# Dense products that read their moving operand, and write their bank, from the last column to the first

## The reference

```
mod = silu(c) @ w_ada + b_ada                       # 2048 x 6144, for the latent and for the context
u   = rms_norm(h) * (1 + scale) + shift             # 256 + 256 tokens
p   = u @ w_in                                      # z, x B C, dt, q k v, beta, alpha
y   = [ssd_scan(conv(xBC)), gdn_scan(conv(qkv))]    # both directions, context state carried to the latent
x   = x + gate * rms_norm(norm_gate(y) @ w_out)
for l in 0, 1:
    h = rms_norm(x); q k v b c i = split(h @ w_in_2[l])          # 2048 x 6144
    x = x + [diff_attention(q, k, v), b * conv3(c * i)] @ w_out_2[l]
    h = rms_norm(x)
    x = x + relu(h @ w_up_2[l])**2 @ w_down_2[l]                 # 2048 x 8192, 8192 x 2048
```

## Time and profile before

| | |
|---|---|
| time, median of 3 runs | 3028.11 us |
| time of the profiled execution | 3026.63 us |
| its span, first to last instruction | 3024.8 us |
| mean granted TensorE clock | 0.995 |
| TensorE matmul (PE) busy | 2981.0 us, 99% |
| weight load (PEld) busy | 2823.5 us, 93% |
| VectorE, ScalarE, GpSimd busy | 62%, 44%, 10% |
| DMA, mean | 181 GB/s |

### The profile page before, as it was taken

The page is one execution under the profiler, slowest core; times in us unless marked ns, Lnnn a source line. Parts: engine busy times, 40 slices in busy tenths (PEclk is TensorE's granted clock), DMA queues, the critical chain, the costliest instruction groups (busy, mean ns, idle before and its releaser), DMA issues.

```text
span 3024.8 us, 68274 instructions
## 1 busy us (share of the span) xinstructions
PE 2981.0 (99%) x28670; PEld 2823.5 (93%) x28670; DVE 1863.7 (62%) x2510; ACT 1333.8 (44%) x1732; POOL 295.3 (10%) x351
## 2 busy tenths in 40 slices
PE   6999999999999999999999999999999999999999
PEld 2688888888989999999999999999999999999999
DVE  3677777688876666555455555566665555555554
ACT  3455455455454444444343333444444443333333
POOL 0000000000111212110010000211122110000000
PEclk8999999999999999999999999999999999999999
DMA  9612212323955454555555555544545555555554
GB/s 398 276 58 85 85 60 83 122 101 113 394 184 203 180 178 174 190 195 192 191 191 192 193 193 195 222 177 172 180 173 189 192 191 191 191 193 193 195 194 153
DMA packets 82964, 547.13 MB, mean 181 GB/s; under 512 B 9125, under 2 KB 13365, under 8 KB 18928
## 3 DMA queue, kind: packets, MB, share of 16 engines
q1 hardware_dynamic: 78448, 523.27, 47.5%
q10 hardware_dynamic: 2192, 15.40, 1.3%
q0 software_dynamic: 2160, 6.05, 0.6%
HBM read 540.46 MB, written 7.36 MB: 181 GB/s over the span
## 4 chain that ended last, share of the span: by engine, by line
PE 95%; DMA 1%; DVE 1%; ACT 1%; PEld 0%; issue 0%; PEldq 0%; POOL 0%; SPq 0%; ACTq 0%; DVEq 0%; POOLq 0%
PE bank L446 29%; PE bank L447 28%; PE bank L448 28%; PE bank L864 1%; DMA raw<-stream 1%; PE bank L731 1%; PE bank L737 1%; PE bank L967 1%; DMA xr<-x_t 1%; PE bank L773 0%; PE bank L950 0%; PE bank L789 0%; PE bank L975 0%; PE bank L1179 0%; DVE rs L1726 0%
## 5 line engine op out<-in xcount | busy, mean ns | idle before, releaser
L425 ACT CAST w_hi<-raw 128x2048 fp32r<-128x2048 f32 x443 | 846.9, 1912 | 1222.0 <-PE bank L448 1221.9
L430 DVE TENSOR_TENSOR w_lo<-raw,w_hi 128x2048 fp32r<-128x2048 f32 x443 | 1020.1, 2303 | 549.5 <-ACT w_hi L425 549.2
L446 PE MATMUL bank<-a_lo,w_hi 128*128 128x256 f32 (+1 forms) x3568 | 1060.3, 297 | 0.5 <-PEq L459 0.3
L447 PE MATMUL bank<-a_hi,w_lo 128*128 128x256 f32 (+1 forms) x3568 | 1034.9, 290 | 0.0
L448 PE MATMUL bank<-a_hi,w_hi 128*128 128x256 f32 (+1 forms) x3568 | 1034.6, 290 | 0.0
L446 PE MATMUL bank<-h_lo,w_hi 128*128 128x256 f32 x3552 | 990.0, 279 | 3.8 <-DVE h_lo L2136 3.8
L447 PE MATMUL bank<-h_hi,w_lo 128*128 128x256 f32 x3552 | 981.5, 276 | 0.0
L448 PE MATMUL bank<-h_hi,w_hi 128*128 128x256 f32 x3552 | 981.4, 276 | 0.0
L446 PEld LDWEIGHTS bank<-a_lo,w_hi 128*128 128x128 f32 x3568 | 672.2, 188 | 24.6 <-DVE g_X L1906 2.7
L448 PEld LDWEIGHTS bank<-a_hi,w_hi 128*128 128x128 f32 x3568 | 670.1, 188 | 17.1
L447 PEld LDWEIGHTS bank<-a_hi,w_lo 128*128 128x128 f32 x3568 | 671.3, 188 | 12.2
(11 more groups left out here) (360 smaller groups left out, 2273.8 us busy)
## 6 DMA issues: line engine op xcount, KB each, us to landing
raw<-stream SPq DMA_DIRECT2D x485, 1024.0 KB, 4.8
gate_raw<-stream ACTq DMA_DIRECT2D x12, 1024.0 KB, 7.9
xr<-x_t SPq DMA_DIRECT2D x4, 1024.0 KB, 16.3
q_raw<-stream SPq DMA_DIRECT2D x8, 512.0 KB, 9.6
x_res<-x_t SPq DMA_DIRECT2D x1, 2048.0 KB, 16.6
bias_table<-bias SPq DMA_DIRECT2D x1, 2048.0 KB, 11.1
bias<-bias_table ACTq DMA_DIRECT2D x1, 2048.0 KB, 11.2
out_t<-x_res SPq DMA_DIRECT2D x4, 512.0 KB, 5.0
```

The source lines that it names most:

```text
L425: act.copy(w_hi[u.slot][:], raw[u.raw][:]).then_inc(hi_ready, 1)
L430: dve.tensor_tensor(w_lo[u.slot][:], raw[u.raw][:], w_hi[u.slot][:], ALU.subtract).then_inc(lo_ready, 1)
L446: pe.matmul(acc, wh, lo[:, k, 0:n], start=(k == first), stop=False)
L447: pe.matmul(acc, wl, hi[:, k, 0:n], start=False, stop=False)
```

## The change

`unit_mm` and the quarters of the small unit hand TensorE their moving operand and their bank through `backward`, an access pattern that begins at the last of the n columns and steps by -1. Column j of the operand still meets column j of the bank; the weights, their loads, the order of the matmuls and every wait are as before. The constants `U_SKEW`, `A_SKEW` and `H_SKEW`, all 192 bytes, replace `SKEW`, and name a place for each layer's operands; with these values every operand of a layer has the address it had. Three other things move: the spare weight tiles and the two `gate_raw` buffers that share their place begin 320 bytes later, at a multiple of 512, and `cs` (the 32 columns of silu(c), written once) goes to the end of the arena.

```diff
-SKEW = 48
+U_SKEW = 192
+A_SKEW = (192, 192)
+H_SKEW = (192, 192, 192, 192)
...
-        gate_raw = [put(f"gate_raw{k}", D, at=4 * (RAW * D + 2 * SPL * D + SKEW + KT * T + KT * L + k * D)) for k in range(2)]
+        gate_raw = [put(f"gate_raw{k}", D, at=X_RES - 4 * (2 - k) * D) for k in range(2)]
         for w, g in ((w_hi, 0), (w_lo, 1)):
-            w.append(put(f"w_spare{g}", D, F32R, at=4 * (RAW * D + 2 * SPL * D + SKEW + KT * T + KT * L + g * D)))
+            w.append(put(f"w_spare{g}", D, F32R, at=X_RES - 4 * (2 - g) * D))
...
+        def backward(x):
+
+            (step, rows), (one, n) = x.ap
+            return bass.AP(x.tensor, x.offset + (n - 1) * one, [[step, rows], [-one, n]])
+
...
-            acc = psum[u.bank][:, 0:n]
+            acc = backward(psum[u.bank][:, 0:n])
...
-                pe.matmul(acc, wh, lo[:, k, 0:n], start=(k == first), stop=False)
-                pe.matmul(acc, wl, hi[:, k, 0:n], start=False, stop=False)
-                last = pe.matmul(acc, wh, hi[:, k, 0:n], start=False, stop=(k == final))
+                xl, xh = backward(lo[:, k, 0:n]), backward(hi[:, k, 0:n])
+                pe.matmul(acc, wh, xl, start=(k == first), stop=False)
+                pe.matmul(acc, wl, xh, start=False, stop=False)
+                last = pe.matmul(acc, wh, xh, start=False, stop=(k == final))
...
-                acc = psum[u.bank][:, 0:n]
+                acc = backward(psum[u.bank][:, 0:n])
...
-                    pe.matmul(acc, wh, u_lo3[:, k, 0:n], start=(k == 0), stop=False)
-                    pe.matmul(acc, wl, u_hi3[:, k, 0:n], start=False, stop=False)
-                    last = pe.matmul(acc, wh, u_hi3[:, k, 0:n], start=False, stop=(k == KT - 1))
+                    xl, xh = backward(u_lo3[:, k, 0:n]), backward(u_hi3[:, k, 0:n])
+                    pe.matmul(acc, wh, xl, start=(k == 0), stop=False)
+                    pe.matmul(acc, wl, xh, start=False, stop=False)
+                    last = pe.matmul(acc, wh, xh, start=False, stop=(k == KT - 1))
```

More of the change, by code:

```diff
@@ L268, in build @@
         w_lo = [put(f"w_lo{s}", D, F32R) for s in range(SPL)]
[L269 to L273, removed]
+        A0 = top["at"]
+        u_hi, u_lo = (put(n, KT * T, F32R, at=A0 + U_SKEW + 4 * KT * T * k) for k, n in enumerate(("u_hi", "u_lo")))
+        a_hi, a_lo = ([put(n, KT * T, F32R, at=A0 + skew + 4 * KT * T * k) for skew in A_SKEW] for k, n in enumerate(("a_hi", "a_lo")))
+        top["at"] += 4 * (P + 2 * KT * T)
+        cs = put("cs", 2 * KT, at=4 * (53200 - T - HALF - 2 * KT))
         X_RES = top["at"]
@@ L354, in build @@
         top["at"] = shared
-        h_hi = put("h_hi", KT * L, F32R)
-        h_lo = put("h_lo", KT * L, F32R)
+        H0 = shared - 192
+        h_hi, h_lo = ([put(n, KT * L, F32R, at=H0 + max(skew, 192 + (skew - 192) % 512) + 4 * KT * L * k) for skew in H_SKEW]
+                      for k, n in enumerate(("h_hi", "h_lo")))
+        top["at"] += 4 * 2 * KT * L + max((skew - 192) % 512 for skew in H_SKEW)
         mo = put("mo", KT * L, at=shared + 4 * KT * L)
-        bias = put("bias", 2 * HEADS * L, at=4 * (RAW * D + 2 * SPL * D + SKEW + KT * L))
+        bias = [put("bias", 2 * HEADS * L, at=A0 + skew + 4 * KT * L) for skew in A_SKEW]
         n_sq, n_acc, n_ln, n_rs = (put(n, L) for n in ("n_sq", "n_acc", "n_ln", "n_rs"))
@@ L445, in unit_mm, with mixed3, normed3 @@
                 wh, wl = (w[u.slot][:, k * P:(k + 1) * P] for w in (w_hi, w_lo))
[L446 to L448 removed]
+                xl, xh = backward(lo[:, k, 0:n]), backward(hi[:, k, 0:n])
+                pe.matmul(acc, wh, xl, start=(k == first), stop=False)
+                pe.matmul(acc, wl, xh, start=False, stop=False)
+                last = pe.matmul(acc, wh, xh, start=False, stop=(k == final))
             if part[1] == KT:
                 last.then_inc(unit_done, 1)
[L452 to L454 removed]
+        u_hi3, u_lo3 = (a[:].rearrange("p (k t) -> p k t", t=T) for a in (u_hi, u_lo))
+        def mixed3(l):
+            return (a[l][:, 0:KT * L].rearrange("p (k t) -> p k t", t=L) for a in (a_hi, a_lo))
+        def normed3(m):
+            return (a[m][:].rearrange("p (k t) -> p k t", t=L) for a in (h_hi, h_lo))
         def leave(eng, k):
@@ L1577, in weighted_hi @@
                 tile = ds(i * (4 * L) + j * L, L)
-                act.mul(h_hi[:, tile], x_res[:, tile], par(name, i * 4 + (l * KT + j))).then_inc(S["h_hi_ready"], 1)
+                act.mul(h_hi[m][:, tile], x_res[:, tile], par(name, i * 4 + (l * KT + j))).then_inc(S["h_hi_ready"], 1)
             norm_root(0)
@@ L1675, in turn_ @@
                             tile = i * (4 * L) + ((q % 2) * KT + j) * L
-                            act.copy(a_hi[:, ds(tile, L)], hbuf[:, (2 + j % 2) * L:(3 + j % 2) * L]).then_inc(S["hi_relu"], 1)
+                            act.copy(a_hi[l][:, ds(tile, L)], hbuf[:, (2 + j % 2) * L:(3 + j % 2) * L]).then_inc(S["hi_relu"], 1)
                         elif not isinstance(i, int) or u.c + i * 4 + 2 < N_SEQ:
@@ L2135, in weighted_lo @@
                 tile = ds(i * (4 * L) + j * L, L)
-                stt(h_lo[:, tile], x_res[:, tile], par(name, i * 4 + (l * KT + j)), h_hi[:, tile], ALU.mult, ALU.subtract
+                stt(h_lo[m][:, tile], x_res[:, tile], par(name, i * 4 + (l * KT + j)), h_hi[m][:, tile], ALU.mult, ALU.subtract
                     ).then_inc(S["h_ready2"], 1)
@@ L2275, in turn_ @@
                             tile = ds(i * (4 * L) + ((q % 2) * KT + j) * L, L)
-                            tt(a_lo[:, tile], hbuf[:, (2 + j % 2) * L:(3 + j % 2) * L], a_hi[:, tile], ALU.subtract
+                            tt(a_lo[l][:, tile], hbuf[:, (2 + j % 2) * L:(3 + j % 2) * L], a_hi[l][:, tile], ALU.subtract
                                ).then_inc(S["mlp_ready"], 1)
```

31 lines of the change are left out of this document (17 added, 14 removed).

## The result

The changed kernel takes 3109.93 us, the median of 4 runs (3109.29 to 3111.96), against 3028.10 us of the kernel before, run beside it (4 runs, 3028.07 to 3029.24). The ratio is 1.027, with an interval from 1.026 to 1.0285. The profiled execution took 3110.09 us, its span is 3108.3 us, 83.5 us more than before. The forecast of 2985 us had the wrong sign; the time lies in the range of 2950 to 3140 only because the range had room for the first rival.

The account below looks back on a forecast made before the run. TensorE's instruction spacings were taken to bound the kernel. Gains of 16.9 + 8.4 + 7.1 + 9.7 + 0.7 = 42.8 us off 3026.6 gave 2983.8, forecast as 2985 us, with an 8-in-10 range of 2950 to 3140.

Parts of the forecast that it names:

- the first rival: All stages: slower because reads side by side are worse, +76 to +123 us; slower in all or part had chance 0.31.
- the moving read of 256 columns: Dense 256-column matmuls: spacing would become 112.4 ns, between the load's own 111.4 and today's best rhythm.
- The term for MLPs and projections: MLPs and projections: 16,896 matmuls going from 113.4 to 112.4 ns, 16.9 us faster.
- w_out_2: Stage `w_out_2`: 1,536 matmuls going from 117.9 to 112.4 ns, 8.4 us faster.
- First layer: First layer: 1,968 matmuls, from a middle of 116 ns, gaining 3.6 ns each, 7.1 us faster.
- 512 columns: Matmuls of 512 columns: half of a 15 ns excess goes from 1,296 of them, 9.7 us faster.
- Bank backward: Bank written from the last column: one column a cycle either way, cost 0.
- the rival of half rate: All dense matmuls: a negative step keeps read or write from one column a cycle, 5.3 ms slower; chance 0.06.
- Spare weights: Spare-weight units: 192 matmuls from 120 to 112.4 ns, 1.5 us, 0.7 of it not counted in other stages.
- side by side is worse: All stages at 117.9 or 120 ns, about 3104 to 3151 us; slower in all or part had chance 0.31.
- the rival of no change: All stages: direction is nothing, only 1 us from the spare weights, 3027 us; within 6 us, chance 0.15.
- The bound of failure: MLPs and projections: the forecast fails if their spacing goes up by more than 2.6 ns.

Follow-up runs that it names:

- e3_one_column_back: Changed kernel, moving operand and bank still backward, but every dense weight load reads the first column of its block 128 times; 3102.81 us.
- e4_one_column_fwd: Changed kernel with moving operand and bank forward, every dense weight load reading the first column of its block 128 times; 3023.00 us.
- e9_lines_of_4: Changed kernel, bank and first layer forward; layer 0 reads 4-column groups first to last, backward inside; layer 1 groups last to first, forward inside; 3065.57 us.
- e2_write_back: Changed kernel with the moving operand read forward again and only the bank written backward; 3018.97 us.
- e11_places_only: Changed kernel with read and write forward, leaving only the moved places of spare weights, `gate_raw` and `cs`; median 3050.73 us of twelve runs, ratio 1.0034.
- e15_relock_two: Changed kernel with reads and writes forward, plus pairs of unused transposes behind the sums of squares, none behind the spare-weights unit; 3026.03 us, ratio 0.999 to kernel before.
- e16_relock_three: Changed kernel, reads and writes forward, plus pairs of unused transposes behind the sums of squares and three behind the spare-weights unit; 3027.45 us, ratio 0.9997 to kernel before.

## Why the prediction was wrong

**What bounds the kernel** was right: the time is the sum of TensorE's spacings. The instructions held (28,670 matmuls in both traces; the dense count leaves out 48 of the small unit, at 256 columns, which changes the sum by 0.2 us or less), no wait was added, stream and split kept up, and the stage differences add up to the span's.

**The step that failed** is the moving read of 256 columns: "I take 112.4, the middle between the load's bound and the best rhythm of today, because two readers that go the same way keep their order". It measured 117.78 in the MLPs. The term for MLPs and projections was -16.9 us and came to +78.9. The reason under it fell too: with a load that doesn't travel the two directions give the same 113.3 and 117.8 (`e3_one_column_back`, `e4_one_column_fwd`). What showed in its place is the order in which the moving read takes its 16-byte groups: last to first costs 4.45 ns a matmul even with no step of -1 (`e9_lines_of_4`). I had inferred from an excess that is gone at half clock, depends on place and has two rhythms that it must be the two operands' relative motion. None of the three says anything on the direction, and I had no row on it. The load does have a part in the dependence on place, as the spare weights show, and it makes the 1.3 ns that the backward projections have on top of 117.8 (`e3_one_column_back`), but not the 4.45.

**`w_out_2`**, forecast 8.4 us faster, moved by 0.4 the other way. I had read 117.9 as a price of direction that the change would remove. It is the slow rhythm of a forward stream, taken up behind the sum of squares and left or kept at the spare unit: gone from there on in both layers of `e2_write_back` and in one layer each of `e11_places_only` and `e15_relock_two`, and behind the three transposes in one layer of `e16_relock_three`.

**First layer**, forecast -7.1, came to +4.7: the same step.

**512 columns**, forecast -9.7, came to +0.3. Here the reading of the row was off as well: the 50 matmuls of the window hold 48 of the unit and two neighbours. From the first to the last start of that unit it is 11.05 us in both traces, /47 = 235.1 ns, not 230. Direction changes next to nothing of it, 233.3 and 233.5 over the stage, and `e3_one_column_back` has 233.5 too; the excess over 213 was not taken apart.

**Bank backward, priced at 0**, was right (`e2_write_back`); the rival of half rate had no support, neither for the read (117.8, not 213) nor for the write. The Trainium skill ("PSUM — Partial Sum Buffer", Specifications) says that a non-contiguous bank pattern slows matmuls; a step of -1 over neighbouring columns is not such a case here, 113.33 ns with it and without it.

**Spare weights**, 1.5 us, came to 0.3: 118.0 instead of 112.4, the lowest level of backward reads.

**The rival that came true** in its number is "side by side is worse" (+76 to +123; measured +82), with all stages at 117.9 or 120 and fewer than 2649 matmuls as its sign. That was luck in part: it took its levels from the slow stretches of a forward read, and the backward read has the same average by another pattern. Its two reasons did not hold: neither the order of two travelling readers nor a place that suits only the present direction, as far as places were tried. Nor is the rival of no change right in saying that direction is nothing. Its ground, that the two reads do not hold each other up, fits the equal price of direction with and without a travelling load; the projections (119.1 and 117.8 ns) and the spare weights (120.0 and 113.3) speak against it.

**The bound of failure**, 2.6 ns more in MLPs and projections, was set too high: the other terms of the forecast give 25.9 us together, and 25.9/16,896 = 1.5 ns. The measured 4.4 and 5.5 are over either.

**What stays open**: why 16-byte groups in falling order cost 32 cycles more for each three matmuls (353.3 against 340 ns, at 2.4 GHz 848 against 816), what fixes the rhythm at a re-entry behind the spare unit, why one turn back in 128 bytes gave 113.3 behind one spare unit and 117.8 elsewhere, how the place of the weights enters, and which way the load reads.

## What to carry to other kernels

In a stream like this one (fp32r, 256 moving columns, a load of 128 beside each) let the moving operand be read in rising order of address at least from one 16-byte group to the next. The order within a group and the direction of the bank's write were free here, so a reversal that an algorithm wants belongs there or in a copy that is hidden. In a stream that PE bounds, compare the spacing of equal instructions stage by stage before costing a change: two levels at one address are a rhythm and no price of the pattern, and a stretch that can run at either needs some repeats before two kernels are compared. Equal averages need not be one cause: look at the distances one by one. A number that is read from a window of 50 instructions is good to one of them; take the distance from first to last start.

## What the runs showed of the hardware

- The moving read of 256 fp32r columns with a load of 128 beside it has, in the MLPs, discrete spacings: 113.33, 116.67, 117.78, 118.33, 118.67 and 120.0 ns, held for hundreds of matmuls. At 113.3 nothing was gained by loads of one column (113.33 in the MLPs of `e4_one_column_fwd`).
- Forward, the place decides which can be had: 113.3 at 192 and 320, 120.0 at 0 and 256, 118.7 at 128 and 384. Places 256 bytes apart agree as far as tried. The place of the weights counts too: activations at 192, spare weights at 192 give 120.0, at 0 they give 113.3 or 117.8.
- At a fast place two rhythms, 113.3 and 117.8, keep themselves until the next break (120.0 was seen once, with loads of one column). In `e11_places_only` the same program took 3022 or 3053 us from one execution to the next; the kernel before, with its spare weights elsewhere, never did in 59 runs.
- Backward, 117.8 is the lowest in every stage of every such kernel, also where the load stands still and where transposes precede the re-entry. At 192 bytes, with travelling loads, its distances are 115.0, 118.3 and 120.0; those of the slow forward read lie between 117.3 and 118.3.
